# Second block of a two-part transformer kernel: all four gate slabs as three split products, with three early low parts made on GpSimd

## The reference

```python
def reference(...):
    x = first_block(...)          # 2 layers: gMLP + attention, cross attention, 16 experts
    return second_block(x, ...)   # 2 layers of:
...
    n = _rmsnorm(h, attn_norm[l])                       # 256 tokens x 1024
    p = n @ w_in                                        # 1792 shift cols + 416 latent cols + 2048 gate cols
    p_rw, p_mla, gate_a, gate_b = ...                   # the gate columns are the last 2048
    y_a = _rwkv7_time_mix(...) @ w_out_rwkv
    y_b = _mla(...) @ w_out_mla
    merged = jax.nn.sigmoid(gate_a) * y_a + jax.nn.sigmoid(gate_b) * y_b
    h = h + merged @ w_out
    h = h + _conv_ffn(_rmsnorm(h, ffn_norm[l]), ...)
```

## Time and profile before

| | |
|---|---|
| time, median of 3 runs | 2152.17 us (2149.14 to 2154.25) |
| the profiled execution | span 2150.6 us; no time of its own is given beside it |
| PE busy | 1896.7 us, 88% |
| DVE busy | 915.6 us, 43% |
| ACT busy | 705.2 us, 33% |
| POOL busy | 47.3 us, 2% |
| direct gate matmuls, L3168 | 128 records (two for each of 64 instructions), 593 ns median |

### The profile page before, as it was taken

One profiled execution on the slowest core, in us unless ns is written; L12 is line 12 of the kernel. 1 busy time (PEld: TensorE's weight loads), 2 busy tenths in 40 slices (PEclk: granted clock), 3 DMA queues, 4 the chain that ended last, 5 costly groups with the idle time before them and its releaser, 6 DMA issues.

```text
span 2150.6 us, 37589 instructions
## 1 busy us (share of the span) xinstructions
PE 1896.7 (88%) x16744; PEld 1282.8 (60%) x16744; DVE 915.6 (43%) x1340; ACT 705.2 (33%) x1023; POOL 47.3 (2%) x68
## 2 busy tenths in 40 slices
PE   9999968877768999866766689999999999999998
PEld 7897314332224785312222248677999886779996
DVE  6644201001104754101101137458676574486774
ACT  6644100000003643211111135325544453255443
POOL 2000000000000100000000000000000000000000
PEclk9999989999989999988888899999999999999999
DMA  9266999999999367999999995032853360238540
GB/s 340 98 252 254 420 423 423 425 425 424 428 428 380 120 242 325 427 428 429 428 429 429 429 400 199 4 125 95 265 196 137 123 228 4 92 107 276 185 159 20
DMA packets 142207, 592.53 MB, mean 276 GB/s; under 512 B 5840, under 2 KB 59296, under 8 KB 116720
## 3 DMA queue, kind: packets, MB, share of 16 engines
q1 hardware_dynamic: 140960, 586.68, 68.9%
q0 software_dynamic: 1104, 3.70, 0.5%
HBM read 589.30 MB, written 1.05 MB: 275 GB/s over the span
## 4 chain that ended last, share of the span: by engine, by line
PE 63%; DMA 27%; DVE 4%; ACT 2%; SPq 1%; issue 1%; DVEq 0%; POOL 0%; POOLq 0%; ACTq 0%
PE ps L654 36%; DMA ring<-in_w_up 27%; PE ps L1638 10%; PE ps L3168 3%; PE ps L3217 1%; PE ps L1672 1%; PE ps L1682 1%; PE ps L671 1%; DVE ring_lo L630 1%; PE ps L1567 1%; DMA area<-in_mem 1%; ACT slab_hi L625 1%; PE ps L1211 1%; PE ps L3315 1%; PE ps L3414 0%
## 5 line engine op out<-in xcount | busy, mean ns | idle before, releaser
L1638 PE MATMUL ps<-ring,area 128*32 128x512 f32 x1728 | 275.8, 688 | 154.0 <-DMA ring<-in_w_up 154.0
L630 DVE TENSOR_TENSOR ring_lo<-ring,slab_hi 128x2048 fp32r<-128x2048 f32 (+2 forms) x137 | 302.8, 2213 | 182.4 <-ACT slab_hi L625 182.3
L625 ACT ACTIVATE slab_hi<-ring 128x2048 fp32r<-128x2048 f32 (+2 forms) x137 | 253.3, 1851 | 254.3 <-PE ps L654 237.8
L1638 PEld LDWEIGHTS ps<-ring,area 128*32 128x32 f32 x1728 | 64.8, 124 | 323.5 <-DMA ring<-in_w_up 185.5
L654 PE MATMUL ps<-hT_hi,slab_hi 128*128 128x256 f32 x832 | 234.6, 282 | 0.5 <-DVE ring_lo L630 0.5
L654 PE MATMUL ps<-hT_hi,ring_lo 128*128 128x256 f32 x832 | 233.1, 280 | 0.0
L654 PE MATMUL ps<-hT_lo,slab_hi 128*128 128x256 f32 x832 | 232.9, 280 | 0.0
L2020 ACT ACTIVATE area<-ps 128x512 f32<-128x512 f32 x32 | 19.1, 597 | 548.3 <-PE ps L1638 507.6
L2662 DVE COPY area<-ps 128x256 f32<-128x256 f32 x32 | 13.6, 424 | 411.7 <-PE ps L1543 411.7
L1672 PE MATMUL ps<-ring,area 128*32 128x512 f32 x984 | 122.3, 617 | 55.6 <-DVE area L2693 31.0
L654 PEld LDWEIGHTS ps<-hT_hi,slab_hi 128*128 128x128 f32 x832 | 156.7, 188 | 1.3 <-DVE ring_lo L630 1.1
(11 more groups left out here) (494 smaller groups left out, 3302.7 us busy)
## 6 DMA issues: line engine op xcount, KB each, us to landing
ring<-in_w_down SPq DMA_DIRECT2D x59, 2048.0 KB, 25.5
ring<-in_w_up SPq DMA_DIRECT2D x58, 2048.0 KB, 21.2
ring<-in_w_gate SPq DMA_DIRECT2D x56, 2048.0 KB, 15.7
ring<-in_w_ffn_up SPq DMA_DIRECT2D x44, 1024.0 KB, 8.3
ring<-in_w_in SPq DMA_DIRECT2D x18, 2048.0 KB, 12.8
ring<-in_w_ffn_down SPq DMA_DIRECT2D x10, 2048.0 KB, 8.0
area<-in_w_gate SPq DMA_DIRECT2D x6, 2048.0 KB, 12.9
ring<-in_xattn_w_kv SPq DMA_DIRECT2D x4, 2048.0 KB, 17.1
```

Of the source, the lines that this page charges most:

```text
L625: return m.nc.scalar.activation(hi, whole, ACT.Copy)
L630: return m.nc.vector.tensor_tensor(lo, whole, hi, ALU.subtract)
L1638: ins = mm(ps[32 * g:32 * g + CAP, 1, :], m.tokT[:, k, :], rows[:, (g % 2) * BANK:(g % 2 + 1) * BANK], start=k == 0, stop=k == KD - 1)
```

## The change

All 64 gate steps of a layer become split products. The rows are `m.n1_hi` and `m.n1_lo` themselves, which stay where they are until the last step: n1_hi moves to the memory of `m.hT`, the whole copy moves to the area of C and E1 (still made, for L2903 alone), and `gate_rows_split` goes. ACT makes the high parts of the first three halves (slab 0, and the first half of slab 1) in the input stage, behind the tile copies of q = 5, 6, 7; POOL makes their low parts, ahead of its latent root. The fourth half takes the place of the row split on ACT and DVE. The step order within slabs 0 and 1 becomes that of slabs 2 and 3. The split of `H_OUT2` moves behind the last sigmoid on ACT and behind the rotation on DVE.

```diff
@@ signals, memory
-             ("gate_hi", 5), ("gate_lo", 5), ("gates_half", 1)):
+             ("early_gate_hi", 3), ("early_gate_lo", 3), ("gate_hi", 5), ("gate_lo", 5)):
-    m.n1_hi = over("n1_hi", area_at, after_lat + 5 * PAIRS * T, KD, T)
+    m.n1_hi = over("n1_hi", hT_at, 0, KD, T)
+    m.n1 = view(KD, T, at=after_lat + 3 * PAIRS * T)
-    m.gate_hi = over("gate_hi", extra_at, 0, SLAB // 2)
+    m.gate_hi = (over("gate_hi0", area_at, 16384, SLAB // 2), over("gate_hi1", area_at, after_lat + 5 * PAIRS * T, SLAB // 2),
+                 over("gate_hi2", extra_at, 0, SLAB // 2))
@@ gates
-EXACT_GATES = 2
+EARLY_GATES = 3
 def gate_step(i):
     j, r = i // (2 * KD), i % (2 * KD)
-    if j < EXACT_GATES:
-        return j, r // KD, r % KD
     return j, r // 4 % 2, r // KD * 4 + r % 4
 def gate_half(m, j, h):
     slot, half = PLAN2[W_GATES + j].slot, slice(h * (SLAB // 2), (h + 1) * (SLAB // 2))
-    room = m.ring_lo[:, PLAN2[W_GATES + 1].slot]
-    hi = m.gate_hi[:, :] if (j, h) in ((2, 0), (3, 1)) else room[:, 0:SLAB // 2] if j == 2 else room[:, SLAB // 2:]
+    n = 2 * j + h
+    if n < EARLY_GATES:
+        hi = m.gate_hi[n][:, :]
+    elif n == 5:
+        hi = m.gate_hi[2][:, :]
+    else:
+        freed, part = ((0, 0), (0, 1), None, (1, 0), (1, 1))[n - EARLY_GATES]
+        hi = m.ring_lo[:, PLAN2[W_GATES + freed].slot, part * (SLAB // 2):(part + 1) * (SLAB // 2)]
     return hi, m.ring_lo[:, slot, half], m.ring[:, slot, half]
@@ tensor_rwkv, fill
-            if j < EXACT_GATES:
...
-                ins = mm(out, m.hT[:, k, tokens], w[:, k, :], start=k == 0, stop=k == KD - 1)
+            half = 2 * j + k // 4
+            if k % 4 == 0 and t == 0:
+                if half < EARLY_GATES:
+                    wait("early_gate_lo", half + 1)
+                else:
+                    wait("gate_lo", half - EARLY_GATES + 1)
+            w = [a.rearrange("p (k n) -> p k n", n=BANK)[:, k % 4, :] for a in gate_half(m, j, k // 4)[:2]]
+            first, ins = exact(m, out, [a[:, k, tokens] for a in (m.n1_hi, m.n1_lo)], w, k == 0, k == KD - 1)
@@ scalar_second, in the loop over SHIFT_ORDER
+        if 5 <= q < 8:
+            n = q - 5
+            landed2(m, act, l, W_GATES + n // 2)
+            high(m, *gate_half(m, n // 2, n % 2)).then_inc(s("early_gate_hi"), 1)
@@ scalar_rwkv
-    wait("n1_whole")
-    high(m, *gate_rows_split(m)).then_inc(s("gate_hi"), 1)
+    high(m, *gate_half(m, 1, 1)).then_inc(s("gate_hi"), 1)
...
-    wait("gates_half")
...
+    gate_rows("rest")
     split_first_out()
-    gate_rows("rest")
@@ gpsimd_second
     gpsimd_rstd(m, pool, l, "n1", "n1_sq", 0, NT, 0)
+    for n in range(EARLY_GATES):
+        pool.wait_ge(*at("early_gate_hi", l, n + 1))
+        hi, lo, whole = gate_half(m, n // 2, n % 2)
+        m.nc.gpsimd.tensor_tensor(lo, whole, hi, ALU.subtract).then_inc(s("early_gate_lo"), 1)
     gpsimd_rstd(m, pool, l, "l", "l_sq", 10, 2 * NT, 0)
@@ vector_rwkv, vector_mla
-    low(m, *gate_rows_split(m)).then_inc(s("gate_lo"), 1)
+    low(m, *gate_half(m, 1, 1)).then_inc(s("gate_lo"), 1)
...
-    vector_split2(m, dve, l, H_OUT2)
     wait("h_full")
...
         .then_inc(s("qk2_rot"), 1)
+    vector_split2(m, dve, l, H_OUT2)
     dve.wait_ge(*at("bonus_full", l))
```

More of the change, by code:

```diff
@@ L2902, in tensor_second @@
         for k in range(KD):
-            ins = mm(ps[:, 3 + t, QL:LAT], m.hT[:, k, tokens], keys[:, k, :], start=k == 0, stop=k == KD - 1)
+            ins = mm(ps[:, 3 + t, QL:LAT], m.n1[:, k, tokens], keys[:, k, :], start=k == 0, stop=k == KD - 1)
             if k == 0:
@@ L3127, in gates_done @@
     return sum(gate_step(i)[2] == KD - 1 for i in range(GATE_FILLS[point][1]))
-def gate_rows_split(m):
-    room = m.ring_lo[:, PLAN2[W_GATES].slot]
-    return room[:, 0:SLAB // 2], room[:, SLAB // 2:], m.hT[:, :, :].rearrange("p k n -> p (k n)")
 def gate_half(m, j, h):
     slot, half = PLAN2[W_GATES + j].slot, slice(h * (SLAB // 2), (h + 1) * (SLAB // 2))
-    room = m.ring_lo[:, PLAN2[W_GATES + 1].slot]
-    hi = m.gate_hi[:, :] if (j, h) in ((2, 0), (3, 1)) else room[:, 0:SLAB // 2] if j == 2 else room[:, SLAB // 2:]
+    n = 2 * j + h
[6 more added lines that the diff above has]
+        hi = m.ring_lo[:, PLAN2[W_GATES + freed].slot, part * (SLAB // 2):(part + 1) * (SLAB // 2)]
     return hi, m.ring_lo[:, slot, half], m.ring[:, slot, half]
@@ L3163, in fill @@
                     wait("gates_sig", n - 1)
-            if j < EXACT_GATES:
-                if k == 0 and t == 0:
-                    landed(W_GATES + j)
-                w = slab(m, PLAN2[W_GATES + j].slot, KD, BANK)
-                ins = mm(out, m.hT[:, k, tokens], w[:, k, :], start=k == 0, stop=k == KD - 1)
-            else:
-                if k % 4 == 0 and t == 0:
-                    wait("gate_lo", 2 * (j - EXACT_GATES) + k // 4 + 2)
-                rows = [a.rearrange("p (k n) -> p k n", n=T)[:, k, tokens] for a in gate_rows_split(m)[:2]]
-                w = [a.rearrange("p (k n) -> p k n", n=BANK)[:, k % 4, :] for a in gate_half(m, j, k // 4)[:2]]
-                first, ins = exact(m, out, rows, w, k == 0, k == KD - 1)
-                if j == PAIRS - 1 and k == 0 and t == 0:
-                    first.then_inc(used(W_GATES + j - 1), 1)
+            half = 2 * j + k // 4
[6 more added lines that the diff above has]
+            first, ins = exact(m, out, [a[:, k, tokens] for a in (m.n1_hi, m.n1_lo)], w, k == 0, k == KD - 1)
+            if j == PAIRS - 1 and k == 0 and t == 0:
+                first.then_inc(used(W_GATES + j - 1), 1)
             if k == KD - 1:
                 ins.then_inc(s("gates_full"), 1)
-            elif j == EXACT_GATES and t == 1 and k == 3:
-                ins.then_inc(s("gates_half"), 1)
     def turn(b, src, half):
@@ L3944, in vector_second @@
     dve.wait_ge(*at("n1_cols_d", l))
-    v.tensor_tensor(m.hT[:, :, :], m.n1_hi[:, :, :], m.n1_lo[:, :, :], ALU.add).then_inc(s("n1_whole"), 1)
+    v.tensor_tensor(m.n1, m.n1_hi[:, :, :], m.n1_lo[:, :, :], ALU.add).then_inc(s("n1_whole"), 1)
     dve.wait_ge(*at("n1_spread", l))
```

## The result

The changed kernel takes 2161.26 us (median of 4, 2160.69 to 2163.85), the kernel before beside it on the same chip 2151.64 (4 runs, 2149.14 to 2154.25): ratio 1.0044, 95% interval 1.0032 to 1.0055. It is slower by 9.6 us, where +3.8 was forecast.

What follows compares the result with a forecast made beforehand. PE was taken as the bound (busy 1896.7 of 2150.6 us). Per layer, 5.1 us of hold less 3.2 of PE's saving gave +1.9, two layers +3.8 on a median of 2152.17: 2156.0 us, range 2144.5 to 2161.

Steps and rivals of the forecast that it cites:

- the hold: Input stage: POOL's subtractions block DVE's instructions with two SBUF operands for their whole length; first products 5.1 us late a layer.
- Steps 1 to 3: Input stage, layer 0: POOL's three subtractions alternate with DVE's work; low parts end 1315.4 and 1322.2, L3964 starts 7.0 us late.
- Step 4: Chain to the reciprocal, layer 0: 1.73 us of ACT's wait absorbs part; reciprocal 5.2 us late, first L3199 5.1.
- DVE is not held: Faster rival, input stage: POOL does not block DVE, only PE's saving is left, -6.4 to 2145.8 us; chance 0.24.
- the next seven fills: 3.2 us a layer, 6.4 us in all: Recurrence: five fills of 3 steps and two of 2 get shorter when split, saving 3.2 us a layer.
- the slack of the waits taken as 0: Waits between those fills follow PE's own products with slack; loss bounded by 0 and 1 us a layer, taken as 0.
- the saving of PE does not arrive: Rival, recurrence: fills were cover and shorter ones expose DVE; without a hold 2150 to 2152 us; chance 0.04.
- PE is busy for all 30 us: First part of the recurrence: PE always busy at 2.4 GHz, so every microsecond PE saves can count where nothing else is due.
- From L3194 to the fill behind fourth_wide: Sign in the recurrence: stretch of 29.4 us should take 26.2; shrinking by less than 2 us proves the prediction wrong.
- the high parts fit in ACT's gaps: Input stage: three high parts of 1.92 us a layer on ACT cost 0, bounds 0 and 0.5 us a layer.
- the moved low part: End, output weights: DVE's 2.29 us fits 2.38 us idle behind the rotation; cost 0, bounds 0 and 2.3 us a layer.

Runs made afterwards that it cites:

- e2d: Kernel before plus three idle 128x2048 GpSimd subtractions placed behind VectorE's own shifts, so they meet its two-operand work; TensorE's work unchanged: 2161.1 us.
- e1c: Changed kernel with GpSimd's three early subtractions cut to 2 of 2048 columns, TensorE using the high part in the low part's place: 2152.0 us.
- e2c: Kernel before plus three idle 128x2048 GpSimd subtractions behind rw_scaled, at the moments meant to match the change's own; TensorE's work unchanged: 2152.2 us.
- e3: Changed kernel with GpSimd's three subtractions moved later, into VectorE's one-input work and idle time ahead of the reciprocal: 2153.9 us.
- e6: e3 with two late fill steps moved ahead of L3194 (prep 7 for 5, rows 2 for 3, u_in 1 for 2): 2151.6 us.
- e5c: Kernel before with direct gate products of one of the two token tiles cut into two of 256 columns, 16 more products a layer: 2157.2 us.
- e7: e6 with two more late fill steps moved into the middle of the recurrence (fourth_wide 4, eighth 3, keys 2, block 5): 2156.5 us.
- e8: Kernel before with only the first gate slab split, the second direct, and three more fill steps ahead of L3199, from rows and u_in: 2156.9 us.
- e5: Kernel before with each direct gate product of 512 columns cut into three of 176, 168 and 168, same columns in all: 2158.4 us.

## Why the prediction was wrong

**Right: the hold.** Steps 1 to 3 of the working hold to 0.2 us: 1315.4, 1319.9 and 1322.2 were forecast, 1315.40, 1319.90 and 1322.05 came. POOL takes 4.65 us for 4.5. Step 4 was 0.3 to 0.4 us too high: the reciprocal is 4.8 us late for 5.2, L4136 4.8 for 5.1. e2d puts the price at 8.7 us in both layers (2161.1 to 2152.4) with nothing else changed. That settles the rival "DVE is not held". Held were instructions with two operands from SBUF, not the shifts with one in PSUM; why L2301 was not, beside an instruction of 16 elements, no run here tells. The Trainium skill (SBUF — State Buffer, Who interferes with whom) has this as a lock for the whole instruction between VectorE with two SBUF inputs and GpSimd; for instructions of 1024 and 2048 elements the trace agrees in both directions.

**Wrong: "the next seven fills: 3.2 us a layer, 6.4 us in all", with the slack of the waits taken as 0.** TensorE's products did get cheaper, by what was forecast. Without issue and at full clock the recurrence holds 85.1 - 4.8 = 80.3 us of work (e1c, layer 1), before 84.1 - 0.9 = 83.2. But the recurrence as a whole averages 85.9 us over six layers with the direct fills (before, e2c, e2d) and 85.9 over six with the split ones (after, e1c, e3). Over these layers issue averages 2.3 us with the direct fills and 3.9 with the split ones. The clock takes 0.3 and 1.9 us by the estimate from its mean. What is left is 83.3 and 80.1: the 3.2 us were there, and longer waits for instructions and a lower clock took about half of them each. The prediction had neither as a term. Of the forecast -6.4 us nothing came: -6.4 + 9.6 of hold (2 x 4.8) would have been +3.2, near the +3.8 on record, and +9.6 was measured. The rival "the saving of PE does not arrive" names the outcome and gives the wrong cause: it looked for DVE behind the fills and had 0.04. (The chances as worked out add up to 0.26 for faster and 0.39 for no change, not 0.27 and 0.38.)

**Where it could have been read.** "PE is busy for all 30 us" was taken for "PE's products are the bound". A stop of 0.90 us put down to issue stood in the same timeline at 1386.87, the chain had 1% of issue, and layer 1 of before had 3.3 us of it; I looked at layer 0 only. A line of x128 in 1.29 us beside it is 256 instructions.

**Also missed: the clock.** A shorter fill ahead of a wait that stays makes idle time, here 2.87 us, and TensorE then ran at 1.2 GHz, 1.4 us for the next fill of layer 0. It fell behind stalls as well, so the two causes are tied: a stall can bring a fall, and e6 hints that a fall gives instructions time to catch up. Whether it is a term of its own is not settled, as e6 and e1c point opposite ways.

**The wrong signs that were named.** From L3194 to the fill behind fourth_wide I forecast 26.2 us for 29.4; it is 1380.61 - 1351.78 = 28.8, a shrinkage of 0.5 where less than 2 was to prove me wrong. In it stand 1.4 us of half speed and 0.8 of issue (0.48 and 0.36). What was counted as nothing was nothing: the high parts fit in ACT's gaps, and L4275 starts with 0.18 us of idle time behind the moved low part.

**What stays open**: why a few more instructions (e5c), or the same in another order (e7, e8), cost 5 us while e6 costs none. That the stalls end with the packets tells what TensorE waits for and not how long it will. Part of it may be the clock: the mean granted clock of all their executions was 0.957 to 0.958 in e5c, e7 and e8, as in the change, and 0.961 in before and e6, where 0.001 of the span is 2.2 us at full speed. But e5, as slow, had 0.960. No run here holds the clock and varies the instructions alone.
